# Moving the streamed operand buffers of a two-block transformer kernel by 64 and 128 bytes

## The reference

```python
# first block
h = rmsnorm(x, norm_mix_g); proj = h @ w_in          # q, k, v, z, gates, conv inputs, ...
y_a = short_conv_branch(bg, cg, xv, conv_a_w) @ w_a_out
y_b = gdn_branch(q, k, v, z, a, b, ...) @ w_b_out    # chunked gated delta rule
x = x + (sigmoid(ga) * y_a + sigmoid(gb) * y_b) @ w_o
x = x + conv_ffn(rmsnorm(x, norm_ffn_g), w_up, ffn_conv_w, w_down)
x = rmsnorm(x, norm_final_g)
# second block
xn = rmsnorm_2(x, norm1_g_2)
...                                                  # nine projections xn @ w_in_2
y = sigmoid(gate_a) * (attention @ w_proj_a_2) + sigmoid(gate_b) * (retention @ w_proj_b_2)
x = x + y @ w_out_2
x = x + square(relu(rmsnorm_2(x, norm2_g_2) @ w_up_2)) @ w_down_2
```

## Time and profile before

| | |
|---|---|
| three runs | 1215.78, 1221.56, 1225.92 us |
| profiled execution, its own time | 1218.03 us |
| its span, first to last instruction | 1216.1 us |
| mean granted TensorE clock | 0.990 |
| TensorE matmul busy | 1165.5 us, 96% of the span |
| VectorE, ScalarE, GpSimd busy | 64%, 50%, 25% |

### The profile page before, as it was taken

One profiled execution on the slowest core, in us unless ns is written; L12 is line 12 of the kernel. 1 busy time (PEld: TensorE's weight loads), 2 busy tenths in 40 slices (PEclk: granted clock), 3 DMA queues, 4 the chain that ended last, 5 costly groups with the idle time before them and its releaser, 6 DMA issues.

```text
span 1216.1 us, 22170 instructions
## 1 busy us (share of the span) xinstructions
PE 1165.5 (96%) x9690; PEld 1138.5 (94%) x9690; DVE 781.0 (64%) x847; ACT 609.1 (50%) x700; POOL 305.6 (25%) x175
## 2 busy tenths in 40 slices
PE   5988999999999899999989999999999999999998
PEld 5887999999999899999979999999998999899998
DVE  5997785555355577677658966755565655765453
ACT  4877432243274465455456643442498544543431
POOL 3343364421023134234235520000011010421010
PEclk9988999999999999999999999999999999999999
DMA  6433331123245444554545454333543555455552
GB/s 245 168 119 139 118 139 71 70 70 139 105 155 196 170 173 167 183 193 157 203 139 186 174 190 174 140 134 144 182 155 114 208 193 189 145 213 197 200 184 102
DMA packets 27744, 192.91 MB, mean 159 GB/s; under 512 B 3072, under 2 KB 3072, under 8 KB 4992
## 3 DMA queue, kind: packets, MB, share of 16 engines
q1 hardware_dynamic: 27648, 191.49, 43.7%
HBM read 190.43 MB, written 1.05 MB: 157 GB/s over the span
## 4 chain that ended last, share of the span: by engine, by line
PE 59%; issue 13%; ACT 10%; DVE 8%; POOL 8%; DMA 2%; POOLq 0%; SPq 0%; ACTq 0%; DVEq 0%
PE psS L527 32%; PE psA L527 9%; PE psS L515 6%; POOL t L1548 6%; ACT wh L847 4%; DVE wl L1164 3%; DVE acc L1167 2%; DMA raw<-in_wts 2%; PE psA L659 1%; PE psA L673 1%; DVE Xl L1167 1%; PE psA L677 1%; ACT L831 1%; POOL ss L1548 1%; DVE gdn L1164 1%
## 5 line engine op out<-in xcount | busy, mean ns | idle before, releaser
L1164 DVE TENSOR_TENSOR wl<-raw,wh 128x2048 fp32r<-128x2048 f32 (+1 forms) x174 | 403.8, 2321 | 207.6 <-ACT wh L847 207.0
L847 ACT ACTIVATE wh<-raw 128x2048 fp32r<-128x2048 f32 x176 | 336.5, 1913 | 295.2 <-PE psS L527 145.2
L527 PE MATMUL psS<-Yh,wh 128*128 128x256 f32 x1056 | 304.5, 288 | 13.4 <-DVE Yl L1167 7.9
L527 PE MATMUL psS<-Yl,wh 128*128 128x256 f32 x1056 | 295.9, 280 | 0.0
L527 PE MATMUL psS<-Yh,wl 128*128 128x256 f32 x1056 | 295.8, 280 | 0.0
L527 PE MATMUL psS<-Xh,wh 128*128 128x256 f32 x896 | 265.0, 296 | 20.3 <-DVE wl L1164 13.5
L527 PE MATMUL psS<-Xh,wl 128*128 128x256 f32 x896 | 252.1, 281 | 0.0
L527 PE MATMUL psS<-Xl,wh 128*128 128x256 f32 x896 | 252.1, 281 | 0.0
L527 PEld LDWEIGHTS psS<-Yh,wh 128*128 128x128 f32 x1056 | 200.9, 190 | 19.4 <-issue 9.4
L527 PEld LDWEIGHTS psS<-Yl,wh 128*128 128x128 f32 x1056 | 200.0, 189 | 2.6 <-issue 1.9
L527 PEld LDWEIGHTS psS<-Yh,wl 128*128 128x128 f32 x1056 | 199.7, 189 | 0.0
(11 more groups left out here) (239 smaller groups left out, 2144.1 us busy)
## 6 DMA issues: line engine op xcount, KB each, us to landing
raw<-in_wts SPq DMA_DIRECT2D x176, 1024.0 KB, 4.8
xT<-in_x SPq DMA_DIRECT2D x2, 512.0 KB, 6.3
raw<-in_wts SPq DMA_DIRECT2D x2, 512.0 KB, 7.3
gdn<-in_x SPq DMA_DIRECT2D x1, 1024.0 KB, 6.8
out<-xT SPq DMA_DIRECT2D x4, 256.0 KB, 2.2
xT<-in_sel SPq DMA_DIRECT2D x1, 512.0 KB, 6.3
xf<-in_dr SPq DMA_DIRECT2D x1, 512.0 KB, 5.8
xT<-in_mask SPq DMA_DIRECT2D x1, 384.0 KB, 5.5
```

The lines of the kernel that those rows point to most:

```text
L527: mm = pe.matmul(bank[:, half], a[:, n % 3, p, :], b[:, kk_, :], start=(first and i == 0), stop=(last and i == 2), skip_group_check=True)
L847: act.activation(wh[:, n % 3], raw[:, n % 2], ACT.Copy).then_inc(sem["wh"], 1)
L1164: dve.tensor_tensor(out, a, b, op).then_inc(sem[name], 1)
```

## The change

Two small unused buffers are put in, each of 16 float32 (64 bytes) in every partition: one ahead of Yh and Yl, one ahead of Xh and Xl.

```diff
--- before.py
+++ after.py
@@ -284,9 +284,11 @@
         ss = [sb(f"ss{i}", [P, 2, S]) for i in range(2)]
         small = sb("small", [P, 64])
         rtok = sb("rtok", [P, 2])
+        sb("aside_y", [P, 16])
         Yh, Yl = sb("Yh", [P, KT, S], F32R), sb("Yl", [P, KT, S], F32R)
 
 
+        sb("aside_x", [P, 16])
         with ExitStack() as own:
             Xh, Xl = sb("Xh", [P, KT, S], F32R, own), sb("Xl", [P, KT, S], F32R, own)
         xf = sb("xf", [P, 4096])
```

## The result

The changed kernel takes 1236.93 us in the median of four runs (1235.79 to 1238.36), the kernel before 1218.67 us (1215.59 to 1225.92) beside it. The ratio is 1.0142 with a 95% interval of 1.009 to 1.0194: slower by some 17 us. The profiled execution has an own time of 1235.79 us, 17.8 more than the 1218.03 of before.

The account below looks back on a forecast made before the run. TensorE's matmul pace, a mixture of 113.3 and 117.7 ns, was taken to bound the kernel. All terms were 0, so 1218.0 + 0 = 1218, given at the median of runs as 1221 us, range 1204 to 1240.

Parts of the forecast that it names:

- What bounds the kernel: The pace of the 8,496 matmuls of L527 and L515, a mixture of 113.3 and 117.7 ns each, nearly half and half.
- The step that failed: Y's matmuls, moved to 256 behind the weights: the same two paces as at 192 and 320, cost 0.
- The second step: X, Z and O, moved from 192 to 320 behind the weights: the same two paces, cost 0 per matmul.
- I take 0, since both paces survive in every relation that I can see, and a mixture of half and half can move either way: All streamed matmuls: the mixture of paces is kept, term 0; chance 0.45.
- The kicks: Changes of pace without a pause where blocks streaming X or Z meet blocks streaming Y; could cost or help, no size.
- The bounds: All matmuls fast would save 15 us, all slow would add 17 us, after what other engines absorb.
- The term for the pauses: Eight slow blocks of u1, paced by other engines, take back 1.6 us if all is fast, some 1.5 if slow.
- mostly fast: Rival: the new relations leave the slow pace no place, 15 us less, 1206 us; chance 0.24.
- Mostly slow: Rival: kicks at X to Y boundaries turn fast stretches slow, 17 us more, 1238 us; chance 0.21.
- A third, worse pace for Y: Rival: Y's 4,416 matmuls stay at 122 ns, 29 us more, 1250 us; chance 0.05.
- That the change does nothing at all, since a shift of 64 bytes isn't seen by the memory: Rival for the whole kernel: no effect, the same 1221 us as the forecast; no chance of its own.
- A better pace than either: Rival: streamed matmuls reach 110 ns, 44 us less with some 7 taken back, 1184 us; chance 0.05.

Follow-up runs that it names:

- e12: Kernel before with weights left and Y, X, Z and O moved to 112 behind them modulo 256: 1218.31 us against 1217.38, ratio 1.0009.
- e1: Kernel before with Y alone moved to 256 behind the weights, X, Z and O still 192: 1229.48 us against 1219.02, ratio 1.0095.
- e3: Kernel before with Y, X, Z and O all moved to 256 behind the weights: 1241.43 us, ratio 1.0189.
- e6: Kernel before with Y moved to 0 and X, Z and O to 64 behind the weights: 1236.53 us, ratio 1.0159.
- e9: Small kernel without the model, TensorE alone, 32 streamed operands in 16-byte steps behind the weights: 113.3 ns a matmul at 112, 120.0 at 0.
- e11: TensorE alone as in e9, but in steps of 4 bytes from 96 to 220 behind the weights: 113.3 ns at 112, 120.0 at 108.
- e2: Kernel before with X, Z and O alone moved to 320 behind the weights, Y still 192: 1225.98 us, ratio 1.0068.
- e13: TensorE alone as in e9, with weights and streams both 16 bytes up: 112 at 120.0 ns in nine of ten series, 192 at 113.3.
- e10: Kernel before with the weights moved to 16 modulo 32 and all streams 112 behind them modulo 256: 1239.76 us against 1218.86, ratio 1.0164.
- e4: Kernel before with everything, weights included, moved up by 64 bytes, so that relations stay: 1217.31 us, ratio 0.9989.
- e5: Kernel before with Y moved to 384 and X, Z and O to 448 behind the weights: 1224.89 us, ratio 1.0069.
- e14: Kernel before with X, Z and O alone moved to 112 behind the weights, Y still 192: 1216.32 us against 1219.41, ratio 0.9977.

## Why the prediction was wrong

It gave 1221 us and no change as the likeliest, 1204 to 1240 as the range. The time of 1236.9 is inside the range, but there is a change, a loss of 1.4%, and a slower kernel had 0.24.

**What bounds the kernel** held where the loss arose: the pace of L527 and L515 sets the end, at a full clock, and the busy times of the others don't move. It didn't hold for the 24 blocks from 48 to 72, as e12 shows.

**The step that failed** is "Y (256 behind). No matmul of this shape has that relation here. Its nearest neighbours on both sides, 192 and 320, have the same two paces. I take 0". e1, e3, e6 and e9 show a single pace of 120.0 ns at 256 and at 0, with or without other work beside it, the weights being where they are in this kernel. I had inferred from two points to one between them, for an effect that goes by steps: in e9, 64 is at 117.8, 112 at 113.3 and 128 at 119, and in e11 112 is at 113.3 and 116 at 120 or more. The modulus of 512 was an assumption too (the size of a weight tile's row); e6 and e9 give 256. By that, 256 is no point between 192 and 320 but the relation 0, both operands at the same place.

**The second step**, "So 320 gives the same two paces as 192. Cost: 0 per matmul at either, with an unknown effect on which one is entered", was right in its first half and left the size in the second. 320 has both paces (X at 1061 us ran at 113.2), but Z and O were at 117.8 in all their matmuls in the kernel after and in e2, and X had 411 of some 2,900 distances below 116 ns. e2 prices that at 8.3 us. The rows had said as much: at 320, the weights of L515 had 453 of 636 distances in the slow pace, and I took the presence of both paces for evenness.

**"I take 0, since both paces survive in every relation that I can see, and a mixture of half and half can move either way"** fell with these two.

**The kicks** came, and they go one way. The timelines have eleven boundaries from a block of Y to one of X, Z or O. In the kernel after (from 256 to 320) the pace behind them is 117.8 at all eleven. In e2 (from 192 to 320) it is 117.8 at all eleven too, at four of them from a Y that ran at 113.3. So it is in e6 (from 0 to 64). In e1 (from 256 to 192) it is 113.3 at all eleven. So what carries X, Z and O into 117.8 is that they come to 320 from another relation, whichever of the three paces Y had, and not Y's 120. It isn't a law of the value 320: in before, L515 came to it from Y at 192 with 113.3 ns and kept them (block 93). The one long fast stretch of X at 320, blocks 147 to 152, began in neither kernel at such a boundary but in block 146, behind a pause of 0.79 us, in the kernel after as in e2. "Help the slow stretches that now have none" held only for 192 behind 256. I had weighed the kicks as able to go either way.

**The bounds.** All slow was put at 18.4 us, less 1.5 that others absorb, 17. Measured were 17.8 in the profiled execution, from two errors that cancel: Y's 3,508 at 120.0 and not 117.8 add 7.7 us, the 635 of L515 another 1.3, 411 fast ones of X take 1.8 away (18.4 + 7.7 + 1.3 - 1.8 = 25.6, where the means of the table give 24.5), and the pauses gave back 6.2, not 1.5 (part of it the clock up to block 24). That the total came out near 17 is luck. The term for the pauses was mis-sized by counting eight slow blocks of u1 (of the seven between 443 and 486 us two, 51 and 53, ran mostly at 113.3): the table of block starts shows that the 24 from 48 to 72 take 149.4 to 150.2 us at any of these paces. The same term had made "mostly fast" worth 15 us: with nearly all streams at 113.3, e12 gained nothing, though its reversed products at 120 take a part of that.

**The rivals.** "Mostly slow" (1238, 0.21) gave the time, with the mechanism of the kicks. "A third, worse pace for Y" (0.05) was right that there is one and put it at 122 ns for 29 us; it is 120.0, and Y and L515 make up 16 of the 24.5 us. The price of the one came with the mechanism of the other. "That the change does nothing at all, since a shift of 64 bytes isn't seen by the memory" is excluded by e1 to e3. "A better pace than either" (0.05): nothing is below 113.3 ns in a stretch that lasts, in the relations of e9, e11 and e13 as little as here, so no better pace was found at this shape, and the distance of 109.2 ns that I estimated from the Trainium skill, TensorE: Matmul & The Clock Gate, "Wait — 56ns, not 53.3ns?", was not reached in any. The transposes and the attention's products, 110 and 112 ns apart, were no sign of one: their rows have 128 columns and not 256.

**The rule of the Trainium skill**, SBUF — State Buffer, "Who interferes with whom", by which "PE and ACT never wait on anyone", isn't contradicted if it is read of other engines: e9 has the same paces with nobody beside TensorE, so they are no wait for another. Read as two independent streams of TensorE's own it doesn't hold: e3 costs 1.9% of the whole kernel by addresses alone.

**The spread of the kernel before** (10 us in three runs) I had called a changing mixture. The kernel whose relation has one pace (e3) spreads by 0.7 us in four runs, e10 with nearly one by 2.3 in five, and e12, fast nearly throughout, by 2.0 in eleven. The nearest to two traces of one kernel are before and e4, whose relations are the same. In both, Z has 564 fast distances of 752, O 94 of 94 and L515 182 of 636; but X has 1,651 in before and 1,954 in e4, and Y 1,603 and 2,122. These 822 more, at 4.4 ns, are worth 3.6 us, and e4's span is 2.7 us shorter. A rival is the granted clock. In e5, whose seven runs spread by 6.8 us, the times go by it: 1221.3 and 1221.8 us at a mean of 0.994, 1226.5 to 1228.1 at 0.986 and 0.987. In e14, with 7.7 us in twelve, the quickest had 0.991 and the slowest 0.986, so its spread tells little of the paces. In before it isn't the whole: the two longest of the nine runs beside e10, 1224.1 and 1225.0 us, had 0.994 and 0.992. That the mixture changes from run to run stays argued.

**Left open:** what inside the chip makes the lock, and why the place of both operands counts beside their relation. Common shifts of 16 and 64 bytes were tried, and none of 32.

## What to carry to other kernels

Where TensorE is busy almost without a gap, read its pace as the distance of starts in a window and not as a busy share; one matmul can cost 113.3 or 120.0 ns by nothing but where its two operands lie. Write down where each pair lies modulo 256, treat a relation that the trace doesn't show as unknown and not as the mean of its neighbours, and try the candidates on a small kernel with TensorE alone, with both operands at the addresses modulo 256 that they will have: 112 was good in e9 and e12, and bad in e10, where the weights had moved by 16 bytes. Then count a gain only over blocks that TensorE itself paces: the start of the same block in two kernels tells it, and here 4 to 7 ns in a matmul were worth under 1 us in the 24 blocks of u1 and d1, which a round of three other engines paces.

## What the runs showed of the hardware

Of matmuls with 128x128 loaded and 256 columns streamed, in float32r, at the full clock:

- The start-to-start distance depends on the streamed operand's address less the loaded one's, modulo 256: 120.0 ns at 0, mostly 117.8 at 64, 118.6 to 120.0 at 128, 113.3 or 117.8 at 192 (e1 to e9, loaded tiles at a multiple of 32).
- One layout can hold two stable paces, 113.3 and 117.8, each lasting for hundreds of matmuls, and goes from one to the other at a pause or where the relation changes. For L527's X, Z and O, coming to 64 from another relation gave 117.8 at 33 of 33 boundaries (after, e2, e6), and coming to 192 from 0 gave 113.3 at 11 of 11 (e1); L515 kept 113.3 when it came to 64 (before, block 93).
- The relation isn't all. With weights and streams 16 bytes up together, 112 goes from 113.3 to 120.0 ns (e9, e13; e10 and e12 in the kernel) and 0 from 120.0 to 118.3 in most series, while 192 stays at 113.3; 64 bytes up together changes nothing at 192 (e4).
- It is a matter of single steps: 112 gives 113.3 ns, 108 and 116 give 120 and more (e11).
